# Sums behind the updates, low splits behind them, and the first two weight slots after each layer norm taken together

## What is computed

```python
y = hybrid_mixer(h, ...)                        # ends in the projection w_out
x = layer_norm(ALPHA * x + (1.0 + g1) * y, ln1_g, ln1_b)
h = x * (1.0 + sc2) + sh2
ff = square(relu(h @ w_ff_in)) @ w_ff_out       # 1024 -> 4096 -> 1024
x = layer_norm(ALPHA * x + (1.0 + g2) * ff, ln2_g, ln2_b)
x = x + 0.5 * swiglu_ffn(rms_norm_2(x, ffn1_norm[0]), ffn1_w_in[0], ffn1_w_out[0])
```

## Time and profile before

| | us |
|---|---|
| median of 3 runs | 1720.78 |
| lowest and highest | 1719.75, 1722.82 |
| the profiled execution | 1723.53 |
| its span, first to last instruction | 1721.8 |

### The profile page before, as it was taken

The page is one execution under the profiler, slowest core; times in us unless marked ns, Lnnn a source line. Parts: engine busy times, 40 slices in busy tenths (PEclk is TensorE's granted clock), DMA queues, the critical chain, the costliest instruction groups (busy, mean ns, idle before and its releaser), DMA issues.

```text
span 1721.8 us, 31639 instructions
## 1 busy us (share of the span) xinstructions
PE 1632.2 (95%) x12986; PEld 1591.5 (92%) x12986; DVE 1073.1 (62%) x1557; ACT 828.2 (48%) x1180; POOL 170.4 (10%) x233
## 2 busy tenths in 40 slices
PE   5898999899999899999999999999998989999998
PEld 5898998899999899998999999999997879899998
DVE  7676776687645665566666556665545666666653
ACT  4344545665634544463544444444465445354442
POOL 2002120400201600020100010000100012010000
PEclk9999999999999999999999999999998989999999
DMA  9553591455454454562455464545643004255543
GB/s 369 193 175 120 221 365 52 155 195 197 170 179 165 152 190 160 176 231 98 172 175 191 152 215 173 191 154 179 219 157 142 31 20 152 98 185 177 186 156 123
DMA packets 44837, 293.14 MB, mean 170 GB/s; under 512 B 5168, under 2 KB 6464, under 8 KB 15168
## 3 DMA queue, kind: packets, MB, share of 16 engines
q1 hardware_dynamic: 40896, 265.49, 43.5%
q0 software_dynamic: 3840, 26.23, 3.9%
HBM read 288.02 MB, written 3.67 MB: 169 GB/s over the span
## 4 chain that ended last, share of the span: by engine, by line
PE 74%; DVE 12%; ACT 9%; DMA 2%; issue 2%; POOL 0%; DVEq 0%; ACTq 0%; POOLq 0%
PE G L434 22%; PE G L436 22%; PE G L435 22%; DVE w_lo L1454 4%; ACT w_hi L957 3%; PE O L622 2%; PE T L608 2%; DVE XB L1707 1%; PE L L917 1%; DMA mod_w<-w_ada 1%; DVE X L1574 1%; PE L L810 1%; DVE mod_w L1421 1%; DMA raw<-w_wouta 1%; ACT x_hi L1034 1%
## 5 line engine op out<-in xcount | busy, mean ns | idle before, releaser
L1454 DVE TENSOR_TENSOR w_lo<-raw,w_hi 128x2048 fp32r<-128x2048 f32 (+2 forms) x259 | 546.2, 2113 | 221.1 <-ACT w_hi L957 220.9
L434 PE MATMUL G<-x_hi,w_hi 128*128 128x256 f32 x2176 | 624.9, 287 | 15.1 <-DVE w_lo L1454 10.0
L435 PE MATMUL G<-x_lo,w_hi 128*128 128x256 f32 x2176 | 620.3, 285 | 0.0
L436 PE MATMUL G<-x_hi,w_lo 128*128 128x256 f32 x2176 | 620.0, 285 | 0.0
L957 ACT ACTIVATE w_hi<-raw 128x2048 fp32r<-128x2048 f32 (+1 forms) x261 | 459.3, 1763 | 138.1 <-DMA raw<-w_ffout 43.4
L434 PEld LDWEIGHTS G<-x_hi,w_hi 128*128 128x128 f32 x2176 | 422.3, 194 | 20.2 <-DVE w_lo L1454 11.9
L435 PEld LDWEIGHTS G<-x_lo,w_hi 128*128 128x128 f32 x2176 | 422.2, 194 | 0.1
L436 PEld LDWEIGHTS G<-x_hi,w_lo 128*128 128x128 f32 x2176 | 422.1, 194 | 0.0
L434 PE MATMUL G<-hid_hi,w_hi 128*128 128x256 f32 x1280 | 366.3, 286 | 5.1 <-DVE w_lo L1454 3.1
L436 PE MATMUL G<-hid_hi,w_lo 128*128 128x256 f32 x1280 | 362.7, 283 | 0.0
L435 PE MATMUL G<-hid_lo,w_hi 128*128 128x256 f32 x1280 | 362.6, 283 | 0.0
(11 more groups left out here) (387 smaller groups left out, 1833.1 us busy)
## 6 DMA issues: line engine op xcount, KB each, us to landing
raw<-w_f1in SPq DMA_DIRECT2D x44, 1024.0 KB, 4.8
raw<-w_f2in SPq DMA_DIRECT2D x44, 1024.0 KB, 4.8
raw<-w_f1out SPq DMA_DIRECT2D x32, 704.0 KB, 4.0
raw<-w_f2out SPq DMA_DIRECT2D x32, 704.0 KB, 4.0
raw<-w_ffin SPq DMA_DIRECT2D x16, 1024.0 KB, 4.8
raw<-w_ffout SPq DMA_DIRECT2D x16, 1024.0 KB, 4.8
mod_x<-w_ada POOLq DMA_DIRECT2D x12, 1024.0 KB, 9.0
raw<-w_xk SPq DMA_DIRECT2D x8, 1024.0 KB, 6.1
```

Source lines behind the costliest of these rows:

```text
L434: mm(out, l_hi, r_hi, start=start, stop=False)
L435: mm(out, l_hi, r_lo, start=False, stop=False)
L436: return mm(out, l_lo, r_hi, start=False, stop=stop)
L1454: v.tensor_tensor(w_lo[b][:, 0:s.size], raw[b][:, 0:s.size], w_hi[b][:, 0:s.size].bitcast(F32), ALU.subtract).then_inc(s_lo, 1)
```

## The change

Four things are altered.

1. **Sums.** The sum of the first tiles for the provisional mean is made on VectorE, one add behind each update, instead of on POOL. To that end VectorE's `gated_update` is moved ahead of `splits_to` in the loop over the groups, and the adds stand between them.
2. **Pairs.** Behind each layer norm the first two weight slots are taken together (`gemm_pair`): tile k of slot 0, then tile k - 1 of slot 1, so that each arriving tile feeds four triples. For this both slots must be split before: VectorE makes the quarters of the first during the statistics and those of the second between the tiles of the norm; ScalarE's splits go one slot further ahead, the last of them right before the root of the variance. The filler's result goes to bank `O[1]` with a semaphore of its own, since both `G` banks are in use.
3. **The RMS factor by token.** After the second norm the mean of squares is taken by token (128 x 2), root and reciprocal are taken on two columns, and TensorE spreads the result, which VectorE copies to `R`. TensorE's parts stand inside the pair (`norm_inside`), with four filler triples beside them.
4. **Key copies.** `memory_hi` on ScalarE is spread over the groups instead of standing ahead of them.

```diff
-             {"xsum": 6, "shift": 1, "cent": 8, "sq8": 8, "qsum": 6, "s1": 1, "mu": 1, "s2": 1, "m": 2, "var": 1,
+             {"xsum": 5, "shift": 1, "cent": 8, "sq8": 8, "qsum": 6, "s1": 1, "mu": 1, "s2": 1, "m": 2, "var": 1,
               "c2": 8, "dev": 1, "rt": 1, "rb": 1, "xn": 8, "ax": 1}),
 
     "ffn": ([("ffin", 16), ("f1in0", 22), ("f2in0", 22), ("f1in1", 22), ("f2in1", 22)],
             {k: None for k in ("sg", "h", "hi", "lo")}),
+
+    "tok": ([("ln2", 1), ("end", 1)], {"rt": 1, "rb": 1}),
...
-        if name != "pool":
+        if name not in ("pool", "xk1a", "xk1b"):
...
-                pe.wait_ge(q(name + ".xsum"), nth(name + ".xsum", tiles))
+                pe.wait_ge(q(name + ".xsum"), nth(name + ".xsum", tiles - 1))
                 mm(L[0][:, 0:S], ones_d[:], acc[:], start=True, stop=True).then_inc(q(name + ".shift"), 1)
...
-                        slot_begins(s, 0, s.j0, 0, 4)
+                        slot_begins(s, 0, None, 0, 4)
+                        if turn:
+                            pe.wait_ge(q("k1_ev"), turn)
                         pe.wait_ge(q("m1.lo"), KC * (turn + 1))
                     for both in range(done[0], done[0] + count):
                         f, k = divmod(both, KC)
-                        last = mm3(G[s.j0 % 2][:, f * S:(f + 1) * S], wh[:, k, f, :], wl[:, k, f, :],
+                        last = mm3(O[1][:, f * S:(f + 1) * S], wh[:, k, f, :], wl[:, k, f, :],
                                    m1h[turn][:, k, :], m1l[turn][:, k, :], k == 0, k == KC - 1)
...
+            moments("wout", s, 2, 4, filling("xk1a", 0), 2 * KC - 6)
+
+            def gemm_pair(s, ready, inside):
+
+                for step in range(KC + 1):
+                    for slot in range(2):
+                        k, n, j = step - slot, s.n0 + slot, s.j0 + slot
+                        if not 0 <= k < KC:
+                            continue
+                        if k == 0:
+                            slot_begins(s, slot, j, 0, 4)
+                        if slot == 0:
+                            pe.wait_ge(q(ready), nth(ready, k + 1))
+                        if inside:
+                            inside(slot, k)
+                        wh = w_hi[n % RING][:, :].rearrange("p (k f c) -> p k f c", k=KC, f=2)
+                        wl = w_lo[n % RING][:, :].rearrange("p (k f c) -> p k f c", k=KC, f=2)
+                        for f in range(2):
+                            last = mm3(G[j % 2][:, f * S:f * S + S], wh[:, k, f, :], wl[:, k, f, :],
+                                       x_hi[:, k, :], x_lo[:, k, :], k == 0 and f == 0, k == KC - 1 and f == 1)
+                        if k == KC - 1:
+                            last.then_inc(s_mm, 1)
+
+            def ffn_in(s, ready, after_first=None, pair=False, inside=None):
+                if pair:
+                    gemm_pair(s, ready, inside)
+                else:
+                    gemm_a(s, 0, s.j0, x_hi, x_lo, ready=ready)
                     after_first()
-                for slot in range(1, 4):
-                    gemm_a(s, slot, s.j0 + slot, x_hi, x_lo, between=in_second if slot == 1 else None)
+                for slot in range(2 if pair else 1, 4):
...
+            ffn_in(st["ffin"], "ln1.lo", pair=True)
             ffn_out(st["ffout"], "ffin.lo", HID1, 2, "ffout")
-            moments("ffout", st["ffout"], 1, 6, filling("xk1b", 1))
+            fill = filling("xk1b", 1)
+            moments("ffout", st["ffout"], 1, 6, fill, 6)
+
+            def norm_inside(slot, k):
+                if (slot, k) == (0, KC - 1):
+                    fill(2)
+                    pe.wait_ge(q("ln2.acc"), nth("ln2.acc", KC))
+                    by_token(T[0], acc, True, True).then_inc(q("ln2.mean"), 1)
+                    fill(2)
+                elif (slot, k) == (1, KC - 2):
+                    pe.wait_ge(q("ln2.rt"), nth("ln2.rt", 1))
+                    for t in range(2):
+                        last = mm(O[0][:, t * P:(t + 1) * P], bc(RT[:, t:t + 1], [P, P]), ident[:], start=True, stop=True)
+                    last.then_inc(q("ln2.rb"), 1)
...
+                    ffn_in(st[f"f{f}in{l}"], before + ".lo", pair=True, inside=norm_inside)
...
             def layer_norm(name, s, after, nf, per, tiles, fill, turn):
-                memory_hi(turn)
...
                     splits_to(s.n0 + g * per + per - 1 + AHEAD)
+                    memory_hi(turn, range(min(KC, 3 * g), min(KC, 3 * g + 3)) if turn == 0 else
+                              range(min(KC, max(0, 2 * g - 2)), min(KC, 2 * g)))
...
+                splits_to(fill.n0 + AHEAD + 1)
                 act.wait_ge(q(name + ".var"), nth(name + ".var", 1))
                 act_(dev[:, 2:4], dev[:, 2:4], ACT.Sqrt, bias=eps1[:]).then_inc(q(name + ".dev"), 1)
                 for ft in range(KC):
                     act.wait_ge(q(name + ".xn"), nth(name + ".xn", ft + 1))
                     after(ft)
-                    if ft == 5:
-                        result(fill, 0)
-                        act_(k1[turn][:], tiles2(G[fill.j0 % 2]), ACT.Copy).then_inc(s_ev[fill.j0 % 2], 1)
+                if name != "wout":
+                    root("ln2", T[0][:, 0:2], eps2, out=RTs[:])
+                result(fill, 0)
+                act_(k1[turn][:], tiles2(O[1]), ACT.Copy).then_inc(q("k1_ev"), 1)
...
-                    splits_to(s.n0 + g * per + per - 1 + AHEAD)
                     if g == tiles // nf:
                         dve.wait_ge(q(name + ".shift"), nth(name + ".shift", 1))
                         for ft in range(KC):
...
                     if g >= tiles // nf:
                         dve.wait_ge(q(name + ".cent"), nth(name + ".cent", g * nf + nf))
                     gated_update(s, g, nf, per, gate0)
+                    for ft in range(max(1, g * nf), g * nf + nf):
+                        if ft < tiles:
+                            taken(dve, s.j0 + g)
+                            if ft > 1:
+                                dve.wait_ge(q(name + ".xsum"), nth(name + ".xsum", ft - 1))
+                            v.tensor_tensor(acc[:], X[:, 0, :] if ft == 1 else acc[:], X[:, ft, :], ALU.add)\
+                                .then_inc(q(name + ".xsum"), 1)
+                    splits_to(s.n0 + g * per + per - 1 + AHEAD)
+                for part in range(2):
+                    next_split(0, part)
...
                     if ft >= 2:
                         lo(ft - 2)
+                    if ft >= 4:
+                        next_split(1, ft - 4)
                 lo(KC - 2)
                 lo(KC - 1)
-                next_split(2)
-                next_split(3)
...
+            dve.wait_ge(q("ln2.root"), nth("ln2.root", 1))
+            v.reciprocal(RT[:], RTs[:]).then_inc(q("ln2.rt"), 1)
+            dve.wait_ge(q("ln2.rb"), nth("ln2.rb", 1))
+            own(v.tensor_copy(R[:], O[0][:, 0:S]))
...
-                for ft in range(tiles):
-                    taken(pool, s.j0 + ft // nf)
-                    added(name + ".xsum", ft, acc, X[:, ft, :], ft == 0)
                 for ft in range(KC - 2):
                     pool.wait_ge(q(name + ".sq8"), nth(name + ".sq8", ft + 1))
                     if ft >= tiles:
-                        added(name + ".xsum", ft, acc, X[:, ft, :], ft == tiles)
+                        added(name + ".xsum", ft - 1, acc, X[:, ft, :], ft == tiles)
```

39 lines of the change are left out of this document (17 added, 22 removed).

## The result

The changed kernel is **slower**: 1740.21 us median of 4 runs (1738.29 to 1742.47) against 1720.26 (1718.57 to 1722.82, 4 runs), a ratio of 1.0115 with a 95% interval of 1.0097 to 1.0133. The forecast was 1740.9. The total came out right and its main term too, but two other terms, the filler's clock and the second norm, were off by 2 to 3 us each, and parts of the program that the sum did not contain gave that back.

What follows compares the result with a forecast made beforehand. TensorE, busy 95% of the span, was taken as the bound, so its gaps and following clock falls decide. Terms -4.8, -0.3, +17.0, +3.0, +3.0, +9.0, -6.8 sum to +20.1 us; 1720.8 becomes 1740.9, range 1729.7 to 1749.5.

Steps and rivals of the forecast that it cites:

- the filler's clock: Filler slot behind tile 7 of `ffout`: clock fall after its stall costs only 0.5 us, as small matmuls wait anyway.
- the second norm: From `ffout`'s norm factor to the fourth update in `f1in0`: 29.7 us instead of 36.5, a gain of -6.8 us.
- The stalls in `ffout`: `ffout` tile ends, waiting for low-half splits: slot 2 -0.3, slots 4 to 12 +17.0, slot 14 +3.0, filler +3.0 us.
- The clock term: Behind `ffout`'s stalls at slots 4 to 14: five of six clock falls at 1.7 us, 8.5 of +9.0 us.
- the low halves stay ahead: Rival at `ffout`'s tile ends: update not held, no stalls, the norms' gain stands alone; -14.6 us, 1706; chance 0.04.
- the root's wait: Behind `ffout`, the root waits for a raw tile: 2.1 us by itself, but lying under the filler's delay.
- the stall at slot 2: In `ffout`, the old gap at 466.44 would go if no stalls arise: 3.3 us and 1.8 of clock.
- the first norm: Norm between `wout` and `ffin`: no wait for the provisional mean, paired slots, later root and slot 3; -4.8 us altogether.
- ScalarE's split ahead of the root: First norm: the split of `ffin` slot 2 waits for its raw tile and delays the norm factor, +1.2 us.
- slot 3 of `ffin`: Behind the first norm: VectorE makes slot 3's low half only after the second product, 1.0 us late, +1.0 us.
- The mechanism that I named for slot 3: In `f1in0`: slot 3's raw tile loads only when the filler, now inside the pair, is finished; 0.9 us late.
- The contention with GpSimd: Second norm: quarter splits share a port with GpSimd's sums; costed at nothing, or 0.6 us later last sum by rule.

Runs made afterwards that it cites:

- e3_busy_gaps: The changed kernel with eight triples of unused matmuls ahead of tiles 1 to 7 of `ffout`, inside the stalls: 1735.27 us, ratio 1.0093.
- e1: The changed kernel with VectorE's splits put back ahead of the gated update in `ffout`: 1704.47 us, ratio 0.9917.
- e2: The kernel before with only the order changed: in `ffout`, VectorE makes the gated update ahead of the two splits: 1746.46 us, ratio 1.0170.
- e6_root_first: e1 with ScalarE's split of the second slot behind each norm put behind the root of the variance: 1702.76 us, ratio 0.9900.
- e7_filler_earlier: e6_root_first with eight filler triples ahead of the second norm's pair instead of six, two fewer inside it: 1702.55 us, ratio 0.9895.
- e4: e1 with the second norm's tail undone: no pair in `f1in0`, no factor by token, ten filler triples ahead: 1704.73 us, ratio 0.9911.
- e9: e7_filler_earlier with VectorE's four quarter splits of the second slot moved behind the last low half of x: 1702.71 us, ratio 0.9906.
- e8: The changed kernel with VectorE's running sum in `ffout` moved behind the two splits, the update staying ahead: 1736.42 us, ratio 1.0111.

## Why the prediction was right, and where it was not

**The stalls in `ffout`: right.** Eight, of 2.86 to 3.32 us, at slots 2 to 14 and at the filler, ended by w_lo splits, as listed. With their share of clock the prediction has -0.3 + 17.0 + 3.0 + 8.5 = +28.2 between N1 and U, and the pair's part is -1.2 in the traces (N1 to the end of ffout's slot 1 is 108.5 us where it was 109.7). N1 to U grew by 27.9 and 25.6, so the stalls and their clock cost 29.1 and 26.8. The clock term was 8.5 for five falls at slots 4 to 14, beside the fall at slot 2, which the kernel before has too. The two executions have five and four falls there; e3_busy_gaps, which fills slot 2's stall as well, puts all falls in `ffout` at 8.7 us on average, so some 7.2 without that of slot 2 (1.5). The e1 and e2 runs show the cause itself: the splits behind an update that waits for the second slot of a two-slot tile.

**The rival "the low halves stay ahead" was the right counterfactual.** It gave 1706 for a kernel whose stalls don't arise; e1_split_first, which makes exactly that, took 1704.5. Part of the closeness is again terms that cancel: the root's wait (2.3 us, forecast 2.1) and the stall at slot 2 (4.9, forecast 5.1) are right, but the first norm with its pair gives 6.2 in place of 4.8 and the second 4.5 in place of 6.8.

**The first norm: close.** Forecast -4.8; W to N1 fell by 4.1 us against the profiled execution and by 5.2 against the two others, and with the pair's 1.2 that is -5.3 to -6.4. The wait for the provisional mean went, as said. ScalarE's split ahead of the root was put at +1.2; e6_root_first takes it out and gains 1.08. The step that failed is slot 3 of `ffin`, put at 1.0 us late: no wait of 0.3 us or more stands there.

**The filler: mis-sized.** The stall ahead of it is 2.86 us as forecast (3.0), but its clock term was 0.5 us, "where small matmuls wait anyway". U to N2 grew by 5.0 and 6.0 us, so the clock cost 2.2 and 3.2: the window from 572 to 576 us shows 0.50, the statistics' small matmuls run at half speed (the eight of the squares take 1.70 us where they took 0.95) and VectorE's variance waits for them. The fall also lasts longer here than behind a stall inside `ffout`, at half from 570.3 to 577.1 us in the first execution and from 566.8 to 577.0 in the second. The root's wait lay under this delay, as the prediction says; without the stall it comes out and takes 2.3 us (U to N2 in e1_split_first).

**The second norm: half of what was forecast.** From the norm factor to the fourth update the forecast was 29.7 us in place of 36.5, -6.8. The trace after has 32.28 (576.32 to 608.60), and N2 to Q fell by 3.6. The steps: slot 2 begins at factor + 18.2 where 17.1 was forecast, since the pair reaches its filler at factor + 13.7 and not 12.6: x_lo tiles come late, the fourth behind a quarter of 1.24 us, and the forecast had them all in time; slot 3 begins at factor + 25.7 instead of 23.8, since the filler ends later, at factor + 15.7 and not 14.5, and from there to ScalarE's split of slot 3 it is 5.7 us, not 5.1; and the fourth update follows 6.5 us behind slot 3's first matmul, not 5.9, as VectorE comes to it from its next split without a pause. TensorE's windows show the clock whole from 580 us on. The mechanism that I named for slot 3 is right (e7_filler_earlier), its size was not; and the pair with the factor by token, to which the prediction gave the whole gain, is worth 0.5 us by e4_old_second_norm, as long as slot 3 is late. The contention with GpSimd was costed at nothing, with 0.6 us by the rule, for a late last sum; e9_quarters_behind finds TensorE waiting for that sum neither with the quarters among the additions nor without, and 0.7 us by another path, the quarters ahead of x_lo tiles, of which the contention is a part.

**What cancelled.** Against the mean of the kernel before's three traces, the stretch that the change touches grew by 24.5 and 23.2 us, not 20.1. The rest of the two profiled executions was shorter: W at 312.0 against 315.8 on average, and after Q 1133.9 and 1130.2 against 1133.8. Means of the profiled executions, 1721.6 and 1740.0, differ by 18.4, and that is 23.9 - 3.7 - 1.7 with rounding. The forecast of 1740.9 lies 0.7 us from the median, but its sum was 3 to 4 us short, and parts of the program that the change does not touch made it up: as far as these runs show, that the total fits so well is luck. The range, 1729.7 to 1749.5, would have held the time without that.

**A version that beats both.** e1_split_first, e4, e6, e7 and e9 are all faster than the kernel before, by 0.8 to 1.05%; e7_filler_earlier has the lowest median, 1702.55 us (ratio 0.9895, 0.9871 to 0.9919), and is not told apart from e6 and e9 by time. It also has the shortest W to Q, 254.78, but the 255.52 of e9_quarters_behind hold the fall right behind W (1.5 us); from N1 on e9 is the shortest.

## What to carry to other kernels

A lead of two slots is two slots only as long as what stands between a split and its use does not wait for one of them. Where work is prepared ahead on an in-order engine, count for each group size what a consumer-side wait (here the update, which waits for a tile's *last* slot) holds back: with one slot to a tile the new order cost nothing, with two it cost a full split per tile, and behind most of the stalls a fall of the clock. And measure a change between landmarks that enclose it, in more than one execution: the end-to-end time hid an error of 3 to 4 us in this forecast, and a gain of 4.9 us that another wait had covered.

## What the hardware showed that was not expected

- A stall of 2.8 to 3.3 us was followed by a clock fall in 3 of 7 cases (e2), 4 of 7 (e8), 5 and 6 of 7 (the changed kernel), and in none of 7 where the stall was filled with matmuls (e3). A fall cost 1.4 to 1.6 us in dense matmuls, and 2.4 in the one case in which the clock stood at half for 6.8 us. In the chain of a norm's statistics it stood at half for 6.8 and 10.2 us and cost 2.2 and 3.2, although TensorE does little there.
- Up to the same instruction, executions of one code differ in steps of about 1.6 us (16.9, 18.5 or 20.0 us behind the same wait of 2.96 us), and the part behind Q has two levels, 1130.2 to 1130.4 us in three of fourteen traces and 1133.3 to 1134.6 in the others.
